# A Mamba-2 mixer's raw x turned to channels by VectorE and GpSimd transfers in place of TensorE

## The reference, cut to what matters

```python
def mamba2_mixer(h, w_in, conv_w, conv_b, dt_bias, a_log, d_skip, out_norm_w, w_out):
    zxbcdt = h @ w_in
    z = zxbcdt[..., :D_INNER]                       # D_INNER = 4096
    xbc = zxbcdt[..., D_INNER:D_INNER + CONV_DIM]   # x 4096, B and C 1024 each
    dt = zxbcdt[..., D_INNER + CONV_DIM:]
    xbc = jax.nn.silu(causal_depthwise_conv(xbc, conv_w, conv_b))   # 4 taps along the tokens
    ...
    y = ssd_scan(xs * dt[..., None].astype(xs.dtype), dt * a, bm, cm)   # in chunks of 64 tokens
    y = y + xs * d_skip[:, None].astype(xs.dtype)
    y = gated_group_rms_norm(y.reshape(b, s, D_INNER), z, out_norm_w)
    return y @ w_out
```

## Time and profile before

| | us |
|---|---|
| median of 3 runs | 2415.95 |
| lowest and highest | 2415.84, 2418.39 |
| profiled execution, its own time | 2416.47 |
| its span | 2414.7 |
| TensorE busy | 2404.3 |
| VectorE busy | 1935.6 |
| ScalarE busy | 1284.7 |
| GpSimd busy | 259.9 |

### The profile page before, as it was taken

How to read it: one execution, slowest core, us unless ns; L and a number is a source line. 1 busy time by engine, 2 the same in 40 slices (tenths; PEclk the granted TensorE clock), 3 DMA queues, 4 the chain that set the end, 5 groups by cost and what they waited for, 6 DMA issues and landing times.

```text
span 2414.7 us, 31286 instructions
## 1 busy us (share of the span) xinstructions
PE 2404.3 (100%) x11523; PEld 2004.6 (83%) x11523; DVE 1935.6 (80%) x2107; ACT 1284.7 (53%) x1544; POOL 259.9 (11%) x394
## 2 busy tenths in 40 slices
PE   8999999999999999999999999999999999999999
PEld 7888888888888888888888888888888888888887
DVE  6788888875579889888899866566689898898897
ACT  5555565554455445455555645555555555454453
POOL 1011111111001001011011111110211010010010
PEclk9999999999999999999999999999999999999999
DMA  7777777767778668577677765655887676677684
GB/s 227 217 227 227 226 232 223 230 216 236 220 236 257 213 209 267 172 241 236 197 252 228 238 207 186 189 173 181 259 257 218 219 239 215 225 235 223 195 256 162
DMA packets 288110, 535.35 MB, mean 222 GB/s; under 512 B 22318, under 2 KB 55440, under 8 KB 286976
## 3 DMA queue, kind: packets, MB, share of 16 engines
q1 hardware_dynamic: 264736, 457.87, 59.9%
q0 software_dynamic: 22976, 75.91, 10.9%
q10 hardware_dynamic: 288, 0.11, 0.0%
HBM read 498.09 MB, written 35.72 MB: 221 GB/s over the span
## 4 chain that ended last, share of the span: by engine, by line
PE 67%; issue 25%; DMA 5%; POOL 2%; DVE 2%; ACT 0%; POOLq 0%; ACTq 0%
PE acc L515 9%; PE acc L517 9%; PE acc L516 9%; PE acc L693 7%; PE acc L695 7%; PE acc L694 7%; DMA spread<-work 4%; PE aux L515 2%; PE aux L516 2%; PE aux L517 2%; POOL work L2039 2%; PE aux L532 1%; PE aux L531 1%; PE aux L530 1%; PE aux L719 1%
## 5 line engine op out<-in xcount | busy, mean ns | idle before, releaser
L1085 ACT ACTIVATE w_hi<-w_raw 128x1024 fp32r<-128x1024 f32 x392 | 414.9, 1061 | 494.0 <-PE acc L695 379.6
L1303 DVE TENSOR_TENSOR w_lo<-w_raw,w_hi 128x1024 fp32r<-128x1024 f32 x353 | 427.8, 1221 | 236.8 <-ACT w_hi L894 236.5
L693 PE MATMUL acc<-w_hi,stationary 128*128 128x512 f32 x1564 | 609.9, 390 | 0.0
L694 PE MATMUL acc<-w_lo,stationary 128*128 128x512 f32 x1564 | 609.1, 389 | 0.0
L695 PE MATMUL acc<-w_hi,stationary 128*128 128x512 f32 x1564 | 609.1, 389 | 0.0
L1609 DVE TENSOR_TENSOR w_lo<-w_raw,w_hi 128x1024 fp32r<-128x1024 f32 x392 | 476.3, 1220 | 126.5 <-ACT w_hi L1085 121.0
L894 ACT ACTIVATE w_hi<-w_raw 128x1024 fp32r<-128x1024 f32 x353 | 370.2, 1057 | 299.2 <-PE acc L517 142.4
L515 PE MATMUL acc<-w_hi,stationary 128*128 128x512 f32 x960 | 379.8, 396 | 0.0
L517 PE MATMUL acc<-w_hi,stationary 128*128 128x512 f32 x960 | 374.4, 390 | 0.0
L516 PE MATMUL acc<-w_lo,stationary 128*128 128x512 f32 x960 | 374.2, 390 | 0.0
L693 PEld LDWEIGHTS acc<-w_hi,stationary 128*128 128x128 f32 x1564 | 293.6, 188 | 63.2 <-DVE w_lo L1609 2.9
(11 more groups left out here) (246 smaller groups left out, 2874.0 us busy)
## 6 DMA issues: line engine op xcount, KB each, us to landing
w_raw<-in_w_up SPq DMA_DIRECT2D x200, 512.0 KB
w_raw<-in_w_down SPq DMA_DIRECT2D x192, 512.0 KB
w_raw<-in_ssm_w_in SPq DMA_DIRECT2D x129, 512.0 KB
w_raw<-in_ssm_w_out SPq DMA_DIRECT2D x64, 512.0 KB
work<-in_w_down SPq DMA_DIRECT2D x64, 512.0 KB
w_raw<-in_w_kv SPq DMA_DIRECT2D x64, 512.0 KB
work<-in_w_up SPq DMA_DIRECT2D x56, 512.0 KB
spread<-work POOLq DMA_DIRECT2D x44, 512.0 KB, 4.8
```

The costliest lines, as they stand in the source:

```text
L693: pe.matmul(o, xh, hi[:, k], start=starts[t] and k == 0, stop=False)
L694: pe.matmul(o, xh, lo[:, k], start=False, stop=False)
L1085: a.activation(whi[:, unit % RING, :], raw[:, slot, :], ACT.Copy).then_inc(sem("hi_made"), 1)
L1303: v.tensor_tensor(wlo[:, s, :], raw[:, pos.raw_slot(off), :], whi[:, s, :].bitcast(F32), ALU.subtract).then_inc(sem("lo_made"), 1)
```

## The change

Raw x no longer goes through TensorE and PSUM. Behind piece 15 VectorE turns `xraw` in squares of 32 x 32 into `cvx`; GpSimd stores `cvx` to a new scratch tensor `x_raw` in HBM and loads it back into `xraw` in four transfers, with channels in the partitions. The tokens then lie in 8 blocks of 32, and the convolution treats the edges between the blocks with operations of their own: for each shift one over 8 x 31, 30 or 29 elements, and one over 7 x 1, 2 or 3. ScalarE's four taps and the convolution move behind pieces 0 and 1 of the next group, the later steps of x by one or two pieces, the scan from piece 8 to piece 10, the gate by one piece. The scan's first product goes to the bank `aux[0]` in place of `acc[1]`.

```diff
+        x_raw_tiles = xraw.rearrange("p t c -> p (t c)").rearrange("p (b k i) -> p k b i", k=4, i=32)
@@ TensorE
-            def scan(r):
+            def scan(r, bc):
...
+                pe.wait_ge(sem("bc_read"), bc)
...
-                pe.matmul(acc[1][:, 0, :], cb[:, P:2 * P], xe, start=True, stop=True)
+                pe.matmul(aux[0][:, 0, :], cb[:, P:2 * P], xe, start=True, stop=True)
...
-                    if j == 8 and not first:
-                        scan(g - 1)
+                    if j == 10 and not first:
+                        scan(g - 1, g + 1)
...
-                    if j == 14:
...
-                        transposes(to_channels(aux[1]), lambda i, t: xraw[:, t, i * P:(i + 1) * P]).then_inc(sem("x_raw_turned"), 1)
...
-                if i == 9:
-                    scan(GROUPS - 1)
+                if i == 11:
+                    scan(GROUPS - 1, GROUPS)
@@ ScalarE, tail
+                if j == 0:
+                    a.wait_ge(sem("x_raw_turned"), r * 64 + 64)
+                    for i in range(4):
+                        ct = r * 4 + i
+                        a.activation(squares(cvx[:, i, :]), x_raw_tiles[:, i], ACT.Identity,
+                                     bias=conv_b(ct), scale=conv_w(3, ct)).then_inc(sem("x_tap"), 1)
...
-                if j == 17:
+                if j == 18:
                     a.wait_ge(sem("g_rstd"), r + 1)
@@ VectorE, conv_x
+                for sh in range(1, TAPS):
+                    for edge in (0, 1):
+                        for i in (i0, i0 + 1):
+                            dst, src, w = squares(cvx[:, i, :]), x_raw_tiles[:, i], conv_w(TAPS - 1 - sh, r * 4 + i)
+                            dst, src = (dst[:, 1:, 0:sh], src[:, :7, 32 - sh:]) if edge else (dst[:, :, sh:], src[:, :, 0:32 - sh])
...
+                            ins = v.scalar_tensor_tensor(dst, src, w, dst, ALU.mult, ALU.add)
@@ VectorE, tail
-                if j == 0:
+                if j in (0, 1):
+                    conv_x(r, 2 * j)
+                if j == 2:
                     v.wait_ge(sem("x_tanh"), r * 2 + 1)
...
-                if j == 8:
+                if j == 10:
                     v.wait_ge(sem("x_tokens"), r * 64 + 64)
@@ VectorE, group
+                    if j == 15:
+                        v.wait_ge(sem("x_read"), g + 1)
+                        v.transpose(cvx.rearrange("p i l -> p (i l)").rearrange("p (t q k i) -> p t k q i", t=TT, q=4, k=4),
+                                    xraw.rearrange("p t (k q i) -> p t k q i", k=4, q=4)).then_inc(sem("raw_squares"), 1)
...
-                    if j in (18, 19):
-
-                        conv_x(g, 2 * (j - 18))
@@ GpSimd
+            def x_raw_spread(g):
+
+                gp.wait_ge(sem("raw_squares"), g + 1)
+                gp.dma_start(x_raw_dram.rearrange("t b c q f -> (b c) t (q f)"),
+                             cvx.rearrange("p i l -> p (i l)").rearrange("p (t f) -> p t f", t=TT)).then_inc(sem("x_raw_out"), 16)
+                gp.wait_ge(sem("x_raw_out"), g * 16 + 16)
+                for q in range(4):
+                    gp.dma_start(xraw[32 * q:32 * q + 32].rearrange("c t f -> c (t f)").rearrange("c (b f) -> c b f", f=P),
+                                 x_raw_dram[:, :, :, q, :].rearrange("t b c f -> c (t b) f")).then_inc(sem("x_raw_turned"), 16)
...
                 gp.wait_ge(sem("y_ready"), g)
                 rows_of(g)
+                mask_cb(g)
+                x_raw_spread(g)
                 gate_rstd(g - 1)
-                mask_cb(g)
                 g_out(g - 1)
                 g_back(g - 1)
```

More of the change, by code:

```diff
@@ L599, in scan @@
                 pe.wait_ge(sem("z_read"), r + 1)
-                pe.matmul(acc[1][:, 0, :], cb[:, P:2 * P], xe, start=True, stop=True)
+                pe.wait_ge(sem("bc_read"), bc)
+                if isinstance(r, int) and r == 0:
+                    pe.wait_ge(sem("decays_read"), 1)
+                else:
+                    pe.wait_ge(sem("y_read"), r)
+                pe.matmul(aux[0][:, 0, :], cb[:, P:2 * P], xe, start=True, stop=True)
                 for k in range(HG):
@@ L620, in decays, with group @@
                 mm.then_inc(sem("decays_ready"), 1)
-            def group(g, first):
+            def group(g, first, second=False):
                 pos = Pos(IN0, g, PER_GROUP)
                 for j in range(PER_GROUP):
-                    if j == 0:
-                        if not first:
-                            pe.wait_ge(sem("cb_read"), g)
+                    if j == 0 and not first:
+                        pe.wait_ge(sem("cb_read"), g)
+                        if not second:
+                            pe.wait_ge(sem("off_scaled"), g - 1)
                     if j == 4 and not first:
                         pe.wait_ge(sem("x_read"), g)
[L631 to L635, removed]
+                    if j == 12 and first:
+                        pe.wait_ge(sem("dt_read"), 1)
                     if j < 4:
@@ L657, in group @@
                         pe.matmul(aux[0][:, 1, SEQ:SEQ + P], b[:, P:], c[:, P:], start=True, stop=True).then_inc(sem("cb_ready"), 1)
-                    if j == 14:
[L659 to L663, removed]
-                        transposes(to_channels(aux[1]), lambda i, t: xraw[:, t, i * P:(i + 1) * P]).then_inc(sem("x_raw_turned"), 1)
             group(0, True)
-            with pe.Fori(1, GROUPS) as g:
+            group(1, False, True)
+            with pe.Fori(2, GROUPS) as g:
                 group(g, False)
@@ L991, in group @@
                         start(j)
-                    if j == 4 and not first and not second:
+                    if j == 5 and not first and not second:
                         gate_hi(g - 2)
@@ L1019, in group @@
                     if j == 18:
[L1020 to L1025, removed]
                         a.wait_ge(sem("exponents"), g + 1)
```

51 lines of the change are left out of this document (29 added, 22 removed).

## The result

The changed kernel takes **2434.61 us** (2430.72 to 2437.58, 5 runs), the kernel before 2417.2 in the same comparison: a ratio of 1.0072, 95% interval 1.0061 to 1.0083. It is slower, by 17.4 us where 4.9 were forecast, and 0.6 above the top of the range. The profiled execution's own time is 2434.61 too, 18.1 above that of before.

What follows compares the result with a forecast made beforehand. TensorE's own work was taken as the bound. Waits of 11.4 us in groups 2 to 7 plus 1.4 at the output projection, +12.8, less 7.9 gained, gave +4.9 on 2416.47: about 2421 us, range 2408 to 2434.

Steps and rivals of the forecast that it cites:

- Gain of TensorE, 7.9 us: TensorE without eight transposes a group (7.2 us) and with fewer slow first matmuls at the scan (0.7).
- The rival that the removed work was hidden anyway: Added and removed work both hide: no change, 2416 us; no chance of its own given.
- The chain and its order: From piece 11's end through x's transfer, rsqrt, ScalarE and convolutions: TensorE late 1.2 at piece 2, 1.9 at the scan.
- With a burst of weights in flight, so I take 4.0: GpSimd's store of x until landed: 4.0 us, between 3.5 like the gate's and 5.4 like x's way back.
- a period over 62: Sign that the transfers are wrong: a group period over 62 us, where 60.7 was forecast for groups 2 to 7.
- The rsqrt, taken at 1.5: GpSimd's gate rsqrt behind the x loads: 1.5 us, between 0.73 alone and 2.67 beside VectorE's add.
- Convolution, 3.2 for twelve: VectorE's convolution of two tiles in twelve operations: 3.2 us, bounds 2.4 and 4.8.
- ScalarE's row of 6.9: ScalarE's gate norm, clamp, split of piece 19, exp and split of piece 0, in order after the rsqrt: 6.9 us.
- Way back to the scan: From the squares of x to the scaling, the later of transfer (14.2) and VectorE (14.9); scaling 3.6 to the scan.
- Group 1 doesn't: Group 1 carries no lateness: group 0 has no gate, so no rsqrt; piece 0's split comes 3 us earlier.
- the rival of crowded transfers: Transfers crowd each other: store 5.4 and rsqrt 2.67 make the chain 2.6 longer, +18, 2439 us; chance 0.15.
- the case which the prediction had left open: How often GpSimd's rsqrt meets a VectorE subtraction of 1.2 us; rsqrt then between 0.73 and about 2.

Runs made afterwards that it cites:

- Run 11: Changed kernel without the convolution's six small edge operations, gate mean one piece earlier and rsqrt between x's store and loads: 2409.3 us, 0.9969 of the kernel before.
- run 2: Changed kernel with the six small edge operations of each convolution left out: 2420.8 us, 1.0014 of the kernel before.
- Run 5: Changed kernel with VectorE's reciprocal in place of GpSimd's rsqrt for the gate norm, GpSimd only issuing transfers: 2417.6 us, 1.0004 of the kernel before.
- run 6: Changed kernel with the rsqrt between x's store and loads and VectorE's gate mean one piece earlier, nothing left out: 2419.6 us, 1.0013 of the kernel before.
- run 7: Changed kernel with ScalarE copying x's tiles into flat rows, so VectorE's convolution is six operations again: 2427.1 us, 1.0040 of the kernel before.
- run 3: Changed kernel loading decay rows of one head, not eight, from group 1 on (128 KB for 1 MB): 2432.1 us, 1.0062 of the kernel before.
- run 9: Changed kernel with four weight loads of z shrunk from the second group on: 2428.8 us, 1.0053 of the kernel before.
- run 10: Changed kernel with seven weight loads of z shrunk and decay rows at 128 KB from the second group on: 2421.9 us, 1.0019 of the kernel before.
- run 8: Changed kernel with early gate mean, rsqrt between x's store and loads, and flat x rows with six-operation convolution: 2413.6 us, 0.9983 of the kernel before.
- run 1: Changed kernel with only the rsqrt moved between x's store and its four loads: 2433.9 us, 1.0068 of the kernel before.

## Why the prediction went wrong

- **Gain of TensorE, 7.9 us: right.** Run 11 has no waits in a group and its time is 7.7 below the kernel before; 0.96 a group stands against the 1.0 of the prediction. The rival that the removed work was hidden anyway is out.
- **The chain and its order: right.** ScalarE waits 3.52 for the rsqrt, TensorE for low parts and for the scaling, and both stand where they were forecast. Runs 2, 5, 6 and 7 each shorten another link of it, and each brings time.
- **"With a burst of weights in flight, so I take 4.0": this step failed.** It takes 5.84 in the group shown, more than the upper bound of 5.4 too, because the transfer falls into a stretch in which all DMA engines are taken. Runs 3, 9 and 10 show that it is the crowd: with it gone, 3.5. Part of that crowd are the decay rows: GpSimd issues them at 302.88 and they take 8.1 us to land, so the store starts 7.1 behind them and not 9, while they are still under way (run 3: worth 0.5 of store). The prediction had named a period over 62 as the sign of this error, and it is 62.4. The rows of before had a value for a quiet time and one for a busy time, and I took one near the quiet for a place that I had myself called busy.
- **The rsqrt, taken at 1.5: 0.72.** It came behind VectorE's add, which 1.8 us more of store had seen to. The two errors belong together: 1.84 - 0.78 = 1.06 is the 1.0 that the chain is late at the split of piece 0.
- **Convolution, 3.2 for twelve: 3.24.** ScalarE's row of 6.9: 6.84.
- **Way back to the scan: right in three groups, too short in others.** The prediction let the later of two ways hold, VectorE's own at 14.9. In groups 2, 6 and 7 the scaling waits for nothing and starts 14.9 behind the squares. In groups 1, 3, 4 and 5 it waits 0.15 to 1.57 for the transfer. In the one shown, group 5, it is 357.94 - 342.59 = 15.35, where the prediction had 14.2 for the transfer and so 14.9 in all: 0.45 more. The scaling up to the scan took 3.9 for 3.6. Together with 0.9 from above it makes 1.65 in this group.
- **"Group 1 doesn't": wrong.** Its first scan starts at 112.6 where run 11, without waits, has 110.2: 2.4 late. There no rsqrt is in the way, and ScalarE's taps wait 3.28 for x itself to land, a step that the prediction gave no price. Run 5 without a root has the same 112.6.

```profile
77.64 2.08 ACT L961 ACTIVATE work<-work,params 128x256 f32<-128x256 f32 x4 [3.28 <-DMA work<-x_raw]
```

The sum with these sizes: waits cost 2.4 in group 1 and (437.9 - 414.3) / 7 = 3.4 in each of the seven periods behind it, 26.0 in all, where the prediction had 12.8. The difference, 13.2, is the whole error: 2421.4 + 13.2 = 2434.6. By estimate, with the group shown standing for all, the store less what the rsqrt gave back is 7 x 1.06 = 7.4 of it, group 1 is 2.4, and the remaining 3.4 lies in the way back and the scaling. So the store is the largest error and not the only one: it alone gives 2428.8, inside the range, and run 10 with the store at 3.5 still stands 12.6 above run 11. The range ended at 2434, short of the rival of crowded transfers, and that rival had both of its bounds wrong for this case: a store of 5.4 with an rsqrt of 2.67, where 5.84 and 0.72 came together. The median missed the top by 0.6, less than the 7 us over which single runs spread.

What stays open: run 8 should have come to 2410. Its scans still take 420.1 - 414.3 = 5.8 us more than run 11's, with two waits at scans. One of them (2.09 us, below) is behind x's way back, which took 16.6 us there; no run here changed that transfer. In it GpSimd stood still for 1.46 us between the second load and the third, and the profile shows nothing that it waited for. The same gap stands in the same group of the changed kernel (below) and of runs 6 and 11; its cause stays open.

```profile
351.39 1.09 POOL L2011 DMA_DIRECT2D work<-back  x2 [1.46 <-issue]
```

## What to carry to other kernels

A transfer whose landing a chain waits for is priced by its shape only where the DMA engines have room: read the share of the stretch in which it will stand first, and where it is near 1, take the slowest row that you have as the middle of the bounds and not as their end (here 3.5 us became 5.6 to 6.9). A short operation behind issues on the same queue costs what stands ahead of it, so look for the wait into which it fits, and see that its input is ready by then and that VectorE's long two-input operations are not beside it. Where work moves from the bounding engine to others, the gain is the easy term (here it was right to 0.2 us), and the chain through three engines and a transfer decided.

## What was not expected of the hardware

- The rsqrt of 128x2 took 0.71 where the long add was not beside it, 1.57 when it started 1.29 into the long add, and 2.68 when it started 0.18 into it (runs 6, 10 and 1); both of the last ended 0.58 behind the add, and that of the earlier trace rows 0.56. However late it came into the add, it was held until the add was over. In run 3 it met the subtraction of a low part instead (254.21 to 255.43), took 1.37 from 254.62 on, and ended 0.56 behind it: that is the case which the prediction had left open.
- The first matmul after a wait takes longer: from 331.39 to the next start at 331.62 it is 0.23, the next 0.12.
- In run 8's profile a wait of 2.09 us at one scan was followed by a lower granted clock, 0.69 in the 2 us from 350 on and 0.50 in the next 2, which is 1.2 GHz, while the waits of up to 1.3 in the changed kernel left it at 1.00. The rows are the scan and three stretches around it:

```profile
349.96 1.28 PE L608 MATMUL aux<-work 128*128 128x512 f32 x2 [2.09 <-DVE work L1476]
```
```profile
345.00:350.00 5.00, 2.91 (x14) 2.13 (x12) 3.81 (x11) 3.07 (x4) 0.00 (x0) 1.00 0.40 119
...
350.00:352.00 2.00, 2.00 (x18) 1.06 (x20) 2.00 (x3) 0.00 (x0) 0.00 (x0) 0.69 0.00 0
352.00:354.00 2.00, 2.00 (x43) 2.00 (x40) 2.00 (x3) 0.00 (x0) 0.00 (x0) 0.50 0.51 125
```

The period from that scan to the next (410.36 in the timeline) was 60.4 us, where TensorE's own pace is 58.8, with no wait in it; what the two rows lack of full clock, 0.31 of 2 us and 0.50 of 2 us, makes up the 1.6 (an estimate). The late scaling was paid for twice there. That the wait is what lowered the clock is not shown by a run of its own.
